# The second unit of a sigmoid gate as twelve-bit parts instead of f32, in both layers of a two-part transformer block

## The chip, the cores and the metric

The kernel runs on one core of a Trainium2 chip. The metric is the device time of one execution in microseconds; the runs before the change have a median of 2667.6 us (three runs, 2666.95 to 2668.16).

## The reference, cut to what matters

The input is one sequence of 256 tokens with 1024 channels, in f32. The first block has two layers; each ends in the second of two feed-forwards, to which an embedding term is added behind a gate. A second block with attention and 32 experts follows. The change lies in the line that computes `ple`, and moves work of the line under it.

```python
for i in range(DEPTH):                                  # DEPTH = 2, ALPHA = 4 ** 0.25
    x = layer_norm(ALPHA * x + 0.5 * swiglu(x, ffn1_up[i], ffn1_down[i]), ln1_g[i], ln1_b[i])
    mix = token_mix(x, w_in[i], ...)
    x = layer_norm(ALPHA * x + mix, ln2_g[i], ln2_b[i])
    ple = jax.nn.sigmoid(x @ w_ple_gate[i]) * (p[i] @ w_ple[i])
    x = layer_norm(ALPHA * x + 0.5 * swiglu(x, ffn2_up[i], ffn2_down[i]) + ple, ln3_g[i], ln3_b[i])
return second_block(x, ...)                             # hybrid mixer, then 32 experts, top 4
```

`w_ple_gate` is 1024 x 1024, `w_ple` is 256 x 1024, `ffn2_up` is 1024 x 5632. `swiglu(x, u, d)` splits `x @ u` into a and b and returns `(silu(a) * b) @ d`.

## The kernel before

Activations are held channels by tokens: `x` is 8 chunks of 128 channels by 256 tokens. Weights come in units of 1024 rows by 512 columns (2 MB, two DMAs), which SyncE loads into the two slots of `ring`. TensorE works through numbered groups, one per unit of weights. The groups alternate between two pairs of PSUM banks in `acc`, and a group opens only when its pair has been freed (`acc_free`, in `group_open`). Each engine has its own program, in a fixed order written out by hand; they meet at counting semaphores.

A unit is multiplied in one of two ways. `product` does it in f32: 8 chunks times 4 column blocks of 128, each over 256 tokens. `split_product` does seven of the eight chunks in parts. A weight w is split into a nearer part g (fp32r, twelve bits of it kept) and what is left, l, and a third operand k is made from both; the same is done to x. Three fp32r matmuls then replace one f32 matmul: g by g and l by l into `acc`, k by k into `mix`. The eighth chunk stays in f32 and goes into `mix` first, so that in each half of a unit four f32 records stand ahead of the wait for the parts (`k_ready`).

Three operations make the parts of one half (256 columns) of a unit: ScalarE writes g (`upper`, L1827), VectorE writes l and then k (`lower`, L2233 by way of the helper and L2324). g and k of a half have one place in memory each (`area_parts`, `zz_parts`), so the next unit's half can be split only when TensorE has read this one's; l lies in `ring_parts`, which has two slots like `ring`. The parts of x are made once for a feed-forward, for each half of the tokens: two ScalarE passes (`x_upper`, `x_upper_again`, L1832 and L1835) and two VectorE passes (`x_lower`, `x_sum`, L2331 and L2233). After `split_product`, ScalarE copies `mix` out (`k_summed`), and VectorE joins that copy with `acc` (`join`, L2345).

The stage around the change, in each layer, after the second layer norm:

- TensorE: first unit of the gate by token halves in f32 (`product_halves(PLEG)`, L1316), second unit with `product` (L1317), the embedding's product `p @ w_ple` as two groups (`G_PLE`, L1326), then the eleven units of the second feed-forward (`split_product(L, 1, n)`).
- ScalarE: the layer norm's last step, the four passes over x (L1987 on), the sigmoids of the gate's first unit (L1994), `upper` for both halves of the feed-forward's first unit, the sigmoids of the gate's second unit, then the feed-forward (`silus`). Each of the two blocks of sigmoids ends with `ple_gate`.
- VectorE: the passes over x, `lower` for both halves of the feed-forward's first unit (L2698), then the four multiplications of the embedding's product with the gate (`res`, L2700 on), which free the buffers of the `G_PLE` groups, one large addition (L2708), then the feed-forward (`hidden`).
- SyncE: the gate's second unit is loaded when TensorE is through with the group before the gate. The feed-forward's first unit is loaded when the gate's first is done, its second when the embedding's product is done.

Of the kernel before, what the change touches and what calls it, by code (L numbers as in the profile page):

```python
# [12 lines left out]
ACT = mybir.ActivationFunctionType  # L13
# [28 lines left out]
UP1, DOWN1, PROJ, GATE, MERGE, WOUT, PLEG, PLE, UP2, DOWN2, UNITS = 0, 11, 19, 24, 32, 34, 36, 38, 39, 50, 58  # L42
G_UP1, G_DOWN1, G_PROJ, G_GATE, G_MERGE, G_WOUT, G_PLEG, G_PLE, G_UP2, G_DOWN2, GROUPS = \
# [116 lines left out]
def mixed_blocks(nc, io):  # L160
    CC, NCONST = io["const_cols"], io["consts"].shape[1] - 2048
    ctx = ExitStack()
    with ctx:
# [59 lines left out]
        big = sb("big", [P, 32, T])  # L223
# [177 lines left out]
        k_summed = sem("k_sums_copied")  # L401
        a_joined = sem("a_joined")
# [222 lines left out]
        def bank_done(eng, L, a, b, i=0):  # L625

            eng.wait_ge(acc_done, L * (2 * GROUPS) + (2 * GROUPS + 2 * a + b + 1) + i * 4)
# [9 lines left out]
        def abank(a, b):  # L637
            return acc[:, 2 * (a % 2) + b, :]
# [32 lines left out]


        def parts_made(L, s):
            return 56 * L + (0, 32, 22)[s]

        def half_parts(L, s, n, b):
            return parts_made(L, s) + (2 * n + b + 3 if s == 1 else 2 * n + b + 1)


        def sums_made(L, s):  # L680
            return 50 * L + (0, 28, 20)[s]


        UPS = ((UP1, G_UP1), (UP2, G_UP2))

        def split_unit(s, n):
            return UPS[s][0] + n if s < 2 else (PROJ + n if n < 4 else GATE)

        def split_group(s, n):
            return UPS[s][1] + n if s < 2 else (G_PROJ + n if n < 4 else G_GATE)  # L690


# [8 lines left out]
        def kbank(a, b):  # L701
            return mix[:, 2 * (a % 2) + b, :]
# [257 lines left out]
        def _(pe):  # L960
# [5 lines left out]
            def product(L, r, a, rhs, cols, banks=((0, 1), (2, 3)), nk=DC, i=0, ready=None, uc=UC):  # L966

                group_open(pe, L, a, i)
                w = view(L, r)[:, 0:nk * uc].rearrange("p (k c) -> p k c", c=uc)
                for b, js in enumerate(banks):  # L970
                    for k in range(nk):
                        if b == 0 and k in (0, 4):
                            half_landed(pe, L, r, k // 4, i)
                        if ready is not None and b == 0:
                            ready(k)
                        for n, j in enumerate(js):
                            mm = pe.matmul(abank(a, b)[:, n * T:n * T + T], w[:, k, cols[j]:cols[j] + P], rhs(k),  # L977
                                           start=k == 0 and n == 0, stop=k == nk - 1, skip_group_check=True)
                    mm.then_inc(acc_done, 1)
# [22 lines left out]
            def split_product(L, s, u, i=0):  # L1002

                r, a = split_unit(s, u), split_group(s, u)
                K, wg, wk, xg, xl, xk = PARTS[s]
                group_open(pe, L, a, i)
                w, wl = (m[:, turn_of(L, r) % 2, :].rearrange("p (k c) -> p k c", c=UC) for m in (ring, ring_parts))
                if s == 2:
                    unit_landed(pe, L, r)
                for b in range(2):  # L1010
                    if s < 2:
                        half_landed(pe, L, r, b, i)
                    for c in range(2):
                        c0 = (2 * b + c) * P
                        for k in range(K, DC):
                            pe.matmul(kbank(a, b)[:, c * T:c * T + T], w[:, k, c0:c0 + P], x[:, k, :],  # L1016
                                      start=c == 0 and k == K, stop=False, skip_group_check=True)
                    pe.wait_ge(k_ready, half_parts(L, s, u, b) + i * 4)
                    for c in range(2):
                        c0, ts = (2 * b + c) * P, slice(c * T, c * T + T)  # L1020
                        for k in range(K):
                            pe.matmul(abank(a, b)[:, ts], wg[:, b, k, c * P:c * P + P], xg[:, k, :],  # L1022
                                      start=c == 0 and k == 0, stop=False, skip_group_check=True)
                            pe.matmul(abank(a, b)[:, ts], wl[:, k, c0:c0 + P], xl[:, k, :],  # L1024
                                      start=False, stop=k == K - 1, skip_group_check=True)
                            mm = pe.matmul(kbank(a, b)[:, ts], wk[:, b, k, c * P:c * P + P], xk[:, k, :],  # L1026
                                           start=False, stop=k == K - 1, skip_group_check=True)
                    mm.then_inc(acc_done, 1)
# [223 lines left out]
            for L in range(LAYERS):  # L1252
# [61 lines left out]
                        if h and j == 0:  # L1314
                            half_stats(L, 1, 0, 4, 8)
                product_halves(L, PLEG, G_PLEG, cols, 32, between=lambda: half_stats(L, 1, 1, 4, 8))  # L1316
                product(L, PLEG + 1, G_PLEG + 1, xs, cols)  # L1317
                pe.wait_ge(apart_landed, (L + 1) * 48)
                for hf in range(2):
                    a = G_PLE + hf  # L1320
# [475 lines left out]
        def _(act):  # L1796
# [23 lines left out]


            def upper(L, s, n, hf):
                if s == 2:
                    unit_landed(act, L, split_unit(s, n))
                else:
                    half_landed(act, L, split_unit(s, n), hf)
                act.activation(PARTS[s][1][:, hf], half_unit(L, s, n, hf, ring), ACT.Copy, scale=NEARER).then_inc(g_ready, 1)  # L1827
# [9 lines left out]
            def silus(L, s):  # L1837
                a0, S = UPS[s][1], 2 * L + s
                if S == 0:
                    x_upper(0, 0, 0)  # L1840
                    x_upper_again(0, 0)
                    upper(L, s, 1, 0)
                if s == 0:
                    x_upper(0, 1, 48 * L)
                    x_upper_again(0, 1)
                    upper(L, s, 1, 1)
                    bank_done(act, L, a0, 0)
                    act.activation(silu[:, a0 % 2], abank(a0, 0).rearrange("p (c t) -> p c t", c=2), ACT.Silu).then_inc(silu_ready, 1)
                for n in range(1 - s, 11):
                    a = a0 + n  # L1850
                    bank_done(act, L, a, 0)

                    act.wait_ge(h_ready, S * 11 + n)
                    copy(joined[0], kbank(a, 0).rearrange("p (c t) -> p c t", c=2)).then_inc(k_summed, 1)
                    if n < 10:
                        upper(L, s, n + 1, 0)
                    act.wait_ge(a_joined, 24 * L + (13 + n + 1 if s else n))
                    act.activation(silu[:, a % 2], joined[0], ACT.Silu).then_inc(silu_ready, 1)
                    bank_done(act, L, a, 1)
                    copy(joined[1], kbank(a, 1).rearrange("p (c t) -> p c t", c=2)).then_inc(k_summed, 1)  # L1860
                    if n < 10:
                        upper(L, s, n + 1, 1)
# [41 lines left out]
            for L in range(LAYERS):  # L1904
# [26 lines left out]
                k_sum(1, 1, rk)  # L1931
                k_sum(2, 0, rv)
                k_sum(2, 1, rg)
                act.wait_ge(a_joined, 24 * L + 10 + 1)
                act.activation(rg, rg, ACT.Silu)
                act.drain().then_inc(ret_g, 1)
                k_sum(3, 0, zp[:, 0, :, 16:])
# [5 lines left out]
                for b in range(2):  # L1943
                    k_sum(4, b, big[:, 2 * b:2 * b + 2, :])
                for b in range(2):
                    act.wait_ge(a_joined, 24 * L + 11 + b + 1)
                    act.activation(big[:, 2 * b:2 * b + 2, :], big[:, 2 * b:2 * b + 2, :], ACT.Sigmoid)
                act.wait_ge(s0_var, L + 1)
                act.activation(ml_std, ml_std, ACT.Sqrt).then_inc(s0_std, 1)
# [37 lines left out]
                for h in range(2):  # L1987
                    x_upper(1, h, 48 * L + 24 + 8 * h)
                    x_upper_again(1, h)
                for n in range(2):  # L1990
                    a = G_PLEG + n
                    for b in range(2):
                        bank_done(act, L, a, b)
                        g = act.activation(big[:, 4 * n + 2 * b:4 * n + 2 * b + 2, :],  # L1994
                                           abank(a, b).rearrange("p (c t) -> p c t", c=2), ACT.Sigmoid)
                    g.then_inc(acc_free[a % 2], 1)
                    act.drain().then_inc(ple_gate, 1)
                    if n == 0:
                        for hf in range(2):
                            upper(L, 1, 0, hf)  # L2000
                silus(L, 1)
                if L < LAYERS - 1:
                    layer_norm(L, 2, "ln3_g", "ln3_b")
# [224 lines left out]
        def _(v):  # L2228
# [112 lines left out]
            def join(L, s, n, b, dst):  # L2341
                a = split_group(s, n)
                bank_done(v, L, a, b)
                v.wait_ge(k_summed, sums_made(L, s) + (2 * n + b + 1 if s == 1 else 2 * n + b - 1))
                return v.scalar_tensor_tensor(out=dst, in0=abank(a, b).rearrange("p (c t) -> p c t", c=2), scalar=1.0 + 1.0 / STEP,  # L2345
                                              in1=dst, op0=ALU.mult, op1=ALU.add)

# [135 lines left out]
            for L in range(LAYERS):  # L2483
# [211 lines left out]
                    x_lower(L, 1, h, h + 1)  # L2695
                    x_sum(1, h)
                for hf in range(2):
                    lower(L, 1, 0, hf)  # L2698
                for n in range(2):
                    a = G_PLE + n  # L2700
                    v.wait_ge(ple_gate, L * 2 + (n + 1))
# [481 lines left out]
```

## Time and profile before

| | us |
|---|---|
| median of 3 runs (lowest, highest) | 2667.6 (2666.95, 2668.16) |
| span of the profiled execution | 2664.9 |
| TensorE busy, of it | 2619.3 (98%) |
| VectorE busy | 1116.4 (42%) |
| ScalarE busy | 676.8 (25%) |

The profiled execution's span is 2.7 us under the median of the runs. The profile is of one core. Busy times count matmuls, activations and vector operations; a matmul's end is modelled, and consecutive matmuls overlap, so starts are read rather than durations. The two layers lie at about 30 to 720 us and 720 to 1435 us, the second block's mixer up to about 1740 us, and its experts from there. The gate's second unit begins at 498.5 us in the first layer and 1208.3 us in the second.

### The profile page before, as it was taken

Reading aid. Unit: us, or ns where it says so; the run is one execution under the profiler, and the core shown is the slowest. Engines: PE = TensorE matmul, PEld = TensorE weight load, DVE = VectorE, ACT = ScalarE, POOL = GpSimd, SP = SyncE. Lnnn points to the kernel's source line nnn. Section 1 sums busy time; section 2 is a strip of 40 time slices with the busy share of each in tenths; the row PEclk is TensorE's granted clock in tenths of the full one; section 3 lists DMA queues with packets and bytes.
Section 4 is the critical chain, followed back from the end, with each engine's and each line's share of the span. In section 5 each row is a group of like instructions: output and inputs, shape, how many; then the busy total and the mean of one; then the engine's idle time right before and its main releaser. Section 6 shows DMA issues by size and latency. Waiting matters only on the chain.

```text
span 2664.9 us, 37976 instructions
## 1 busy us (share of the span) xinstructions
PE 2619.3 (98%) x15345; PEld 1912.6 (72%) x15345; DVE 1116.4 (42%) x1589; ACT 676.8 (25%) x1201; POOL 73.5 (3%) x95
## 2 busy tenths in 40 slices
PE   7999999999999999999999999999999999999998
PEld 7999888999999998899989888843333333333333
DVE  5875524586587473156832144321212212112212
ACT  3313320342143042214413043121212121112111
POOL 0000200000100110000001000000000000000000
PEclk9999999999999999999999999999999999999999
DMA  6575333456755842344562643689999999999999
GB/s 229 182 264 205 127 127 142 145 182 205 246 181 175 308 168 96 138 161 143 181 216 97 218 153 141 264 349 427 427 428 428 427 427 428 427 427 428 428 427 414
DMA packets 265072, 705.25 MB, mean 265 GB/s; under 512 B 12932, under 2 KB 155216, under 8 KB 214928
## 3 DMA queue, kind: packets, MB, share of 16 engines
q1 hardware_dynamic: 254464, 664.71, 64.7%
q0 software_dynamic: 9856, 36.41, 3.8%
q10 hardware_dynamic: 656, 2.78, 0.3%
q8 instruction: 69, 1.13, 0.2%
q14 instruction: 27, 0.22, 0.0%
HBM read 699.61 MB, written 6.60 MB: 265 GB/s over the span
## 4 chain that ended last, share of the span: by engine, by line
PE 83%; DMA 9%; SPq 7%; issue 1%; DVE 0%; ACT 0%; DVEq 0%
PE acc L977 12%; PE acc L1065 11%; PE acc L1684 11%; PE acc L1022 6%; PE mix L1026 6%; PE acc L1024 6%; SPq L862 4%; PE acc L1699 4%; PE acc L1504 4%; PE mix L1016 4%; PE acc L994 3%; DMA zp<-in_w 3%; SPq L859 3%; PE acc L1296 2%; DMA big<-in_w 2%; DMA ring<-in_w 2%
## 5 line engine op out<-in xcount | busy, mean ns | idle before, releaser
L1022 PE MATMUL acc<-branch_parts,area_parts 128*128 128x256 f32 x1176 | 344.2, 293 | 0.1
L1026 PE MATMUL mix<-big_parts,zz_parts 128*128 128x256 f32 x1176 | 332.9, 283 | 0.0
L1024 PE MATMUL acc<-area_parts,ring_parts 128*128 128x256 f32 x1176 | 332.5, 283 | 0.0
L1065 PE MATMUL acc<-big,ring 128*128 128x256 f32 (+1 forms) x1408 | 269.7, 353 | 0.0
L1065 PEld LDWEIGHTS acc<-big,ring 128*128 128x128 f32 x1408 | 241.1, 190 | 28.3 <-issue 0.8
L2982 DVE COPY zz<-acc 128x512 f32<-128x512 f32 x32 | 22.1, 692 | 548.8 <-PE acc L1684 548.8
L1022 PEld LDWEIGHTS acc<-branch_parts,area_parts 128*128 128x128 f32 x1176 | 225.1, 191 | 8.9 <-DVE zz_parts L2324 0.5
L1024 PEld LDWEIGHTS acc<-area_parts,ring_parts 128*128 128x128 f32 x1176 | 225.2, 191 | 0.2
L1026 PEld LDWEIGHTS mix<-big_parts,zz_parts 128*128 128x128 f32 x1176 | 225.1, 191 | 0.0
L977 PE MATMUL acc<-x,ring 128*128 128x256 f32 x1024 | 224.3, 380 | 0.0
L977 PEld LDWEIGHTS acc<-x,ring 128*128 128x128 f32 x1024 | 193.8, 190 | 26.7 <-issue 0.3
L2233 DVE TENSOR_TENSOR ring_parts<-ring,area_parts 128x1792 fp32r<-128x1792 f32 x84 | 170.1, 2025 | 48.8 <-ACT area_parts L1827 43.7
L2324 DVE SCALAR_TENSOR_TENSOR zz_parts<-area_parts,ring_parts 128x1792 fp32r<-128x1792 f32 x84 | 170.2, 2026 | 6.3
L1827 ACT ACTIVATE area_parts<-ring 128x1792 fp32r<-128x1792 f32 x84 | 142.3, 1694 | 12.6 <-DMA ring<-in_ffn_up 12.6
L1819 ACT ACTIVATE area<-acc 128x256 f32<-128x256 f32 (+1 forms) x66 | 32.5, 492 | 368.8 <-PE acc L1636 342.8
L1684 PE MATMUL acc<-ring,zz 128*64 128x512 f32 x512 | 117.6, 598 | 5.0 <-DMA ring<-in_w 5.0
L1016 PE MATMUL mix<-x,ring 128*128 128x256 f32 x464 | 116.8, 379 | 0.0
L994 PE MATMUL acc<-x,ring 128*128 128x128 f32 x768 | 90.5, 280 | 16.2 <-DMA ring<-in_ffn_up 16.2
L1684 PE MATMUL acc<-big,zz 128*64 128x512 f32 x432 | 100.8, 596 | 2.8 <-DMA big<-in_w 2.8
L994 PEld LDWEIGHTS acc<-x,ring 128*128 128x128 f32 x768 | 89.9, 197 | 16.4 <-issue 16.1
L1819 ACT ACTIVATE zz<-acc 128x512 f32<-128x512 f32 x66 | 39.3, 597 | 244.5 <-PE acc L1684 196.7
L2233 DVE TENSOR_TENSOR area<-area 128x256 f32<-128x256 f32 (+3 forms) x142 | 62.1, 457 | 79.0 <-PE acc L1699 68.5
(516 smaller groups left out, 3761.2 us busy)
## 6 DMA issues: line engine op xcount, KB each, us to landing
big<-in_w SPq DMA_DIRECT2D x89, 1024.0 KB, 25.6
ring<-in_ffn_up SPq DMA_DIRECT2D x88, 1024.0 KB, 5.0
ring<-in_w SPq DMA_DIRECT2D x84, 1024.0 KB, 25.7
ring<-in_w_in SPq DMA_DIRECT2D x72, 1024.0 KB, 7.1
spare<-in_w SPq DMA_DIRECT2D x42, 1024.0 KB, 25.8
area<-in_w_ada POOLq DMA_DIRECT2D x24, 1024.0 KB, 8.1
tables<-in_w SPq DMA_DIRECT2D x23, 1024.0 KB, 25.6
branch<-in_w SPq DMA_DIRECT2D x23, 1024.0 KB, 25.7
```

The costliest lines, as they stand in the source:

```text
L862: sp.dma_start(wbuf[n].unsqueeze(1), w2[:, bass.ds(e * 4 + k, 1), :]).then_inc(BUFFERS[n][0], 16)
L977: mm = pe.matmul(abank(a, b)[:, n * T:n * T + T], w[:, k, cols[j]:cols[j] + P], rhs(k), start=k == 0 and n == 0, stop=k == nk - 1, skip_gr ...
L994: mm = pe.matmul(abank(a, j // 2)[:, c0:c0 + P], w[:, k, cols[j]:cols[j] + P], x[:, k, half(h)], start=k == 0 and j % 2 == 0, stop=k == DC ...
L1016: pe.matmul(kbank(a, b)[:, c * T:c * T + T], w[:, k, c0:c0 + P], x[:, k, :], start=c == 0 and k == K, stop=False, skip_group_check=True)
L1022: pe.matmul(abank(a, b)[:, ts], wg[:, b, k, c * P:c * P + P], xg[:, k, :], start=c == 0 and k == 0, stop=False, skip_group_check=True)
L1024: pe.matmul(abank(a, b)[:, ts], wl[:, k, c0:c0 + P], xl[:, k, :], start=False, stop=k == K - 1, skip_group_check=True)
L1026: mm = pe.matmul(kbank(a, b)[:, ts], wk[:, b, k, c * P:c * P + P], xk[:, k, :], start=False, stop=k == K - 1, skip_group_check=True)
L1065: mm = pe.matmul(outs[c], w[:, k, c * P:c * P + P], rhs(kk), start=opens[c] and kk == 0, stop=kk == FC - 1, skip_group_check=not all(opens))
L1684: mm = pe.matmul(H_BANK[j // 2][lo:lo + 64, :], x_slot[:, k, :], w[:, j * UC:j * UC + UC], start=k == 0, stop=k == DC - 1)
L1827: act.activation(PARTS[s][1][:, hf], half_unit(L, s, n, hf, ring), ACT.Copy, scale=NEARER).then_inc(g_ready, 1)
L2233: return v.tensor_tensor(out, a, b, op)
L2324: v.scalar_tensor_tensor(out=PARTS[s][2][:, hf], in0=g, scalar=-1.0 / STEP, in1=l.bitcast(F32), op0=ALU.mult, op1=ALU.add) \
```

## The change

The gate's second unit becomes `split_product(L, 1, -1)`: unit -1 of the second feed-forward's stage, with that stage's parts of x. ScalarE makes its nearer parts (`upper(L, 1, -1, hf)`) right after the passes over x, ahead of the sigmoids of the first unit. VectorE makes the lower ones where it made those of the feed-forward's first unit. Its result is copied out by ScalarE, joined by VectorE, and only then put through the sigmoid. The parts of the feed-forward's first unit are made one half at a time, after each half of the gate's unit has been copied (ScalarE) or joined (VectorE). The semaphore counts move by two per layer. No DMA is added or moved.

```diff
         def half_parts(L, s, n, b):
-            return parts_made(L, s) + (2 * n + b + 3 if s == 1 else 2 * n + b + 1)
+            return parts_made(L, s) + (2 * n + b + 5 if s == 1 else 2 * n + b + 1)
...
         def split_unit(s, n):
+            if (s, n) == (1, -1):
+                return PLEG + 1
...
         def split_group(s, n):
+            if (s, n) == (1, -1):
+                return G_PLEG + 1
...
                 product_halves(L, PLEG, G_PLEG, cols, 32, between=lambda: half_stats(L, 1, 1, 4, 8))
-                product(L, PLEG + 1, G_PLEG + 1, xs, cols)
+                split_product(L, 1, -1)
...
                     x_upper(1, h, 48 * L + 24 + 8 * h)
                     x_upper_again(1, h)
-                for n in range(2):
-                    a = G_PLEG + n
-                    for b in range(2):
-                        bank_done(act, L, a, b)
-                        g = act.activation(big[:, 4 * n + 2 * b:4 * n + 2 * b + 2, :],
-                                           abank(a, b).rearrange("p (c t) -> p c t", c=2), ACT.Sigmoid)
-                    g.then_inc(acc_free[a % 2], 1)
-                    act.drain().then_inc(ple_gate, 1)
-                    if n == 0:
-                        for hf in range(2):
-                            upper(L, 1, 0, hf)
+                for hf in range(2):
+                    upper(L, 1, -1, hf)
+                a = G_PLEG
+                for b in range(2):
+                    bank_done(act, L, a, b)
+                    g = act.activation(big[:, 2 * b:2 * b + 2, :], abank(a, b).rearrange("p (c t) -> p c t", c=2), ACT.Sigmoid)
+                g.then_inc(acc_free[a % 2], 1)
+                act.drain().then_inc(ple_gate, 1)
+                a = G_PLEG + 1
+                for b in range(2):
+                    bank_done(act, L, a, b)
+                    copy(big[:, 4 + 2 * b:6 + 2 * b, :], kbank(a, b).rearrange("p (c t) -> p c t", c=2)).then_inc(k_summed, 1)
+                    upper(L, 1, 0, b)
+                for b in range(2):
+                    act.wait_ge(a_joined, 26 * L + 13 + b + 1)
+                    act.activation(big[:, 4 + 2 * b:6 + 2 * b, :], big[:, 4 + 2 * b:6 + 2 * b, :], ACT.Sigmoid)
+                act.drain().then_inc(ple_gate, 1)
                 silus(L, 1)
...
                 for hf in range(2):
-                    lower(L, 1, 0, hf)
+                    lower(L, 1, -1, hf)
+                for b in range(2):
+                    o = join(L, 1, -1, b, big[:, 4 + 2 * b:6 + 2 * b, :])
+                    if b:
+                        o.then_inc(acc_free[(G_PLEG + 1) % 2], 1)
+                    v.drain().then_inc(a_joined, 1)
+                    lower(L, 1, 0, b)
                 for n in range(2):
                     a = G_PLE + n
                     v.wait_ge(ple_gate, L * 2 + (n + 1))
```

## Rows read from the trace of the kernel before

**Rows 1.** The page: busy time of the engines, and the chain by engine

```profile
PE 2619.3 (98%) x15345; PEld 1912.6 (72%) x15345; DVE 1116.4 (42%) x1589; ACT 676.8 (25%) x1201; POOL 73.5 (3%) x95
PE 83%; DMA 9%; SPq 7%; issue 1%; DVE 0%; ACT 0%; DVEq 0%
```

**Rows 2.** Waits of TensorE, 0 to 1400 us: total, times, longest

```profile
PE acc L994 <- DMA ring<-in_ffn_up: 16.2, 1, 16.2
```

**Rows 3.** Windows: stretch, busy time of each engine, clock, DMA share, GB/s

```profile
498.50:512.30 13.80, 13.80 (x66) 12.17 (x66) 7.27 (x5) 4.76 (x5) 0.00 (x0) 1.00 0.44 152
...
1246.80:1258.60 11.80, 11.80 (x94) 11.47 (x93) 10.18 (x8) 4.89 (x5) 0.00 (x0) 1.00 0.53 178
```

**Rows 4.** Waits of SyncE's queue, 1650 to 2665 us

```profile
SPq L862 <- PE acc L1684: 80.3, 41, 4.7
```

**Rows 5.** Timeline of TensorE (start, us, engine, line, operation), both layers

```profile
498.54 13.98 PE L977 MATMUL acc<-x,ring 128*128 128x256 f32 x64
512.36 7.07 PE L1326 MATMUL acc<-ptile,zp 128*128 128x256 f32 x32
519.26 1.03 PE L1016 MATMUL mix<-x,ring 128*128 128x256 f32 x4
519.94 0.47 PE L1022 MATMUL acc<-branch_parts,area_parts 128*128 128x256 f32 x1
520.25 0.28 PE L1024 MATMUL acc<-area_parts,ring_parts 128*128 128x256 f32 x1
...
525.15 1.03 PE L1016 MATMUL mix<-x,ring 128*128 128x256 f32 x4
...
1208.30 13.98 PE L977 MATMUL acc<-x,ring 128*128 128x256 f32 x64
1222.11 7.07 PE L1326 MATMUL acc<-ptile,zp 128*128 128x256 f32 x32
```

**Rows 6.** Timeline of VectorE in the second feed-forward

```profile
529.67 2.03 DVE L2324 SCALAR_TENSOR_TENSOR zz_parts<-area_parts,ring_parts 128x1792 fp32r<-128x1792 f32 x1
...
1247.61 0.69 DVE L2345 SCALAR_TENSOR_TENSOR big<-acc,big 128x512 f32<-128x512 f32 x1 [0.18 <-ACT big L1819]
...
1259.42 0.69 DVE L2345 SCALAR_TENSOR_TENSOR big<-acc,big 128x512 f32<-128x512 f32 x1 [0.18 <-ACT big L1819]
```

**Rows 7.** ScalarE: last pass over x (timeline), and the page's row of nearer parts

```profile
495.32 0.93 ACT L1835 ACTIVATE big_parts<-x 128x896 fp32r<-128x896 f32 x1
...
L1827 ACT ACTIVATE area_parts<-ring 128x1792 fp32r<-128x1792 f32 x84 | 142.3, 1694 | 12.6 <-DMA ring<-in_ffn_up 12.6
```

**Rows 8.** DMA in 40 slices of 480 to 497 us, busy tenths

```profile
DMA  0000001088499999999999400000000000000000
```

**Rows 9.** Timeline of VectorE ahead of the second feed-forward, both layers

```profile
497.94 1.09 DVE L2233 TENSOR_TENSOR big_parts<-branch_parts,area_parts 128x896 fp32r<-128x896 f32 x1
...
505.42 2.03 DVE L2233 TENSOR_TENSOR ring_parts<-ring,area_parts 128x1792 fp32r<-128x1792 f32 x1 [6.38 <-ACT area_parts L1827]
507.52 2.03 DVE L2324 SCALAR_TENSOR_TENSOR zz_parts<-area_parts,ring_parts 128x1792 fp32r<-128x1792 f32 x1
509.46 2.02 DVE L2233 TENSOR_TENSOR ring_parts<-ring,area_parts 128x1792 fp32r<-128x1792 f32 x1
...
514.35 0.69 DVE L2233 TENSOR_TENSOR res<-acc,big 128x512 f32<-128x512 f32 x1 [0.77 <-PE acc L1326]
...
520.25 2.29 DVE L2708 SCALAR_TENSOR_TENSOR res<-res,x 128x2048 f32<-128x2048 f32 x1
...
1208.07 1.09 DVE L2233 TENSOR_TENSOR big_parts<-branch_parts,area_parts 128x896 fp32r<-128x896 f32 x1
```

**Rows 10.** Windows with the clock below 1.00, and at the kernel's start

```profile
1720.00:1732.00 12.00, 12.00 (x58) 10.92 (x58) 0.00 (x0) 1.08 (x2) 0.00 (x0) 0.72 1.01 425
...
16.00:20.00 4.00, 3.82 (x18) 3.85 (x19) 0.00 (x0) 2.09 (x2) 0.00 (x0) 1.00 1.13 420
...
24.00:28.00 4.00, 4.00 (x38) 4.00 (x38) 3.92 (x3) 2.04 (x3) 0.00 (x0) 1.00 0.52 205
```

More of the change, by code:

```diff
@@ L673, in parts_made @@
         def parts_made(L, s):
-            return 56 * L + (0, 32, 22)[s]
+            return 58 * L + (0, 32, 22)[s]
         def half_parts(L, s, n, b):
-            return parts_made(L, s) + (2 * n + b + 3 if s == 1 else 2 * n + b + 1)
+            return parts_made(L, s) + (2 * n + b + 5 if s == 1 else 2 * n + b + 1)
         def sums_made(L, s):
-            return 50 * L + (0, 28, 20)[s]
+            return 52 * L + (0, 28, 20)[s]
         UPS = ((UP1, G_UP1), (UP2, G_UP2))
         def split_unit(s, n):
+            if (s, n) == (1, -1):
+                return PLEG + 1
             return UPS[s][0] + n if s < 2 else (PROJ + n if n < 4 else GATE)
         def split_group(s, n):
+            if (s, n) == (1, -1):
+                return G_PLEG + 1
             return UPS[s][1] + n if s < 2 else (G_PROJ + n if n < 4 else G_GATE)
@@ L1007, in split_product @@
                 w, wl = (m[:, turn_of(L, r) % 2, :].rearrange("p (k c) -> p k c", c=UC) for m in (ring, ring_parts))
-                if s == 2:
+                whole = s == 2 or u == -1
+                if whole:
                     unit_landed(pe, L, r)
                 for b in range(2):
-                    if s < 2:
+                    if not whole:
                         half_landed(pe, L, r, b, i)
@@ L1822, in upper @@
             def upper(L, s, n, hf):
-                if s == 2:
+                if s == 2 or n == -1:
                     unit_landed(act, L, split_unit(s, n))
@@ L1856, in silus @@
                         upper(L, s, n + 1, 0)
-                    act.wait_ge(a_joined, 24 * L + (13 + n + 1 if s else n))
+                    act.wait_ge(a_joined, 26 * L + (15 + n + 1 if s else n))
                     act.activation(silu[:, a % 2], joined[0], ACT.Silu).then_inc(silu_ready, 1)
@@ L1933, in _ @@
                 k_sum(2, 1, rg)
-                act.wait_ge(a_joined, 24 * L + 10 + 1)
+                act.wait_ge(a_joined, 26 * L + 10 + 1)
                 act.activation(rg, rg, ACT.Silu)
@@ L1945, in _ @@
                 for b in range(2):
-                    act.wait_ge(a_joined, 24 * L + 11 + b + 1)
+                    act.wait_ge(a_joined, 26 * L + 11 + b + 1)
                     act.activation(big[:, 2 * b:2 * b + 2, :], big[:, 2 * b:2 * b + 2, :], ACT.Sigmoid)
@@ L2343, in join @@
                 bank_done(v, L, a, b)
-                v.wait_ge(k_summed, sums_made(L, s) + (2 * n + b + 1 if s == 1 else 2 * n + b - 1))
+                v.wait_ge(k_summed, sums_made(L, s) + (2 * n + b + 3 if s == 1 else 2 * n + b - 1))
                 return v.scalar_tensor_tensor(out=dst, in0=abank(a, b).rearrange("p (c t) -> p c t", c=2), scalar=1.0 + 1.0 / STEP,
```

## The prediction

> **What bounds the kernel now.** I read the page's busy shares and its chain first: TensorE is busy 98% of the span and carries 83% of the chain [rows 1]. That doesn't say that every stage is TensorE's, so I read its waits next. Up to 1400 us, which holds both layers with this stage, there is one, the 16.2 us for the first weights [rows 2]. Then the windows of the stage itself: beside the gate's second unit TensorE is busy for all of 13.80 us at a granted clock of 1.00, while VectorE works 7.27 us and ScalarE 4.76; in a unit of the second feed-forward TensorE is busy all the time too [rows 3]. So time taken from TensorE here is taken from the whole, and every pause given to it is added. After 1650 us the expert weights stream; SyncE issues them when TensorE lets it, and waited 80.3 us for it at one line alone [rows 4]. I therefore pass a shift of the layers to the end one to one.
>
> **What the change saves.** It touches one unit in each of two layers. In the plain form the unit is 64 records (each f32 matmul of 256 columns leaves two), from 498.54 to the next group at 512.36: 13.82 us, and 13.81 in the second layer (1208.30 to 1222.11) [rows 5]. In the parts form, a unit of the second feed-forward has the same shape (512 columns, seven of eight chunks as three matmuls each, the eighth in f32). Two like joins stand at 1247.61 and 1259.42: 11.81 us per unit [rows 6], without a pause of TensorE [rows 3]. The saving is 13.81 - 11.81 = 2.00 us per layer, 4.0 in all, if the parts are there when TensorE asks.
>
> **When the parts are there.** The parts of x were made before too, and at the same place, so they cost nothing new; they only become urgent. In layer 0 ScalarE ends its four passes over x at 495.32 + 0.93 = 496.25 and then makes the nearer part of each half of the unit, 1.69 us each [rows 7]: the first is there at 497.9. The unit's weights don't hold it, as the transfers end in slice 24 of 40 of that window, at 490 us [rows 8]. VectorE starts its last pass over x at 497.94 (1.09 us). Operations that don't depend on each other overlap by 0.09 (507.52 + 2.03 against 509.46), so the first lower part begins at 498.95, and the two passes for one half take 507.52 + 2.03 - 505.42 = 4.13 us [rows 9]: the first half's parts are ready at 503.08. TensorE begins the unit at 498.54; four f32 records of the eighth chunk keep it for 0.68 us (519.26 to 519.94) [rows 5], so it asks at 499.22. With 0.1 us for the semaphore and the weight load it goes on at 503.2. In an undisturbed half, the first two part matmuls are 0.31 us apart (519.94 to 520.25) [rows 5] where an even share of 11.81 us leaves about 0.12; the 0.19 falls into the pause. **First pause: 503.2 - 499.22 - 0.19 = 3.8 us.** In layer 1 VectorE's last pass starts at 1208.07 [rows 9], so the parts are ready at 1213.2; TensorE asks at 1208.30 + 0.68 = 1208.98; pause 4.15 us. The second half's parts are ready 4.04 us after the first's (505.42 to 509.46 [rows 9]), at 507.1; TensorE gets to them only near 503.2 + 5.0 + 0.9 = 509: no pause there. I take these values and not zero, because each term is a row of the same instruction on data of the same size; I allow 0.3 us either way for the release.
>
> **What is late after it.** The parts of the second feed-forward's first unit used to be made beside the gate's second unit (from 505.42 on [rows 9]). Now they can start only when the halves of that unit are read, because the nearer and the lowest parts lie in the same memory. Call E the moment when TensorE goes from the unit to the embedding's product. In the feed-forward, a half of a unit is over when the next f32 group begins at 525.15 [rows 5]; copy, nearer part and lower parts of the half that takes its place are done at 529.67 + 2.03 = 531.70 [rows 6], 6.55 us later. So VectorE is at this until E + 6.55. Only then does it come to the embedding's multiplications, which stand behind it in its order. Two of them (0.69 us each [rows 9], overlapped by 0.09) free the buffer at E + 7.9. TensorE has done the embedding's product at E + 6.90 (512.36 to 519.26) [rows 5] and needs that buffer for the feed-forward's first unit. **Second pause: with 0.15 us of release and weight load, E + 8.05 - 6.90 = 1.15 us**, the same in both layers. Behind the late work on VectorE stands also the large addition of 2.29 us [rows 9]: two more multiplications, then it, until about E + 11.6, ahead of the feed-forward's first join near E + 14.8. It costs nothing; if that cover of 3 us were gone, the join would be late by what is missing. ScalarE's sigmoids of the second unit, now behind a join, end about E + 4, before VectorE needs them. Its sigmoids of the first unit come 3.4 us later, at about 502, and the buffer that they free is asked for only after the whole unit: hidden. SyncE's queue is not moved; its next feed-forward loads wait for the same groups and shift with them.
>
> **Sum.** Layer 0: 3.8 + 1.15 - 2.0 = +2.95. Layer 1: 4.15 + 1.15 - 2.0 = +3.3. Together **+6.2 us**: a span of 2664.9 + 6.2 = 2671.1. The runs' median is 2.7 us over the profiled span, so 2667.6 + 6.2 = 2673.8. What this can't price is TensorE's clock after such a pause: apart from the start, no row has it idle for about 4 us. Bounds from the nearest rows: nothing on one side (the feed-forward runs at 1.00 [rows 3]); on the other, the stretch from 1720 to 1732 has a mean clock of 0.72, so 12 x 0.28 / 0.5 = 6.7 us at 1.2 GHz instead of 2.4, which is 3.4 us lost, though a run of small matmuls stood before it and no pause [rows 10]. After the first 16.2 us of idling [rows 2], TensorE left 18 records in 4 us where it later left 38 [rows 10]. I take nothing, as a pause of 4 us is nearer to none than to 16, and keep 3.4 per pause for the range.
>
> The Trainium skill, TensorE: Matmul & The Clock Gate, section "Part 1: The HAM clock gate (the "warmup" mystery)", states that an idle array falls back to half clock until it has been busy again. The kernel's start agrees with it (18 records against 38); the drop near 1725 us came without idling and isn't covered by it. By this rule the long pauses would each be followed by a slow stretch, and the time would be the fourth rival's.
>
> **The rivals.**
> 1. *The parts come in time* (faster). Both pauses would be gone and the full 4.0 us kept: 2663.6. It decides at 499.22 us: VectorE would have to end the first half's lower part 3.9 us earlier. Nothing in the rows lets it, as its pass over x starts late, behind ScalarE's four. Chance 0.03.
> 2. *The second pause is not there* (within 0.2%). It hangs on the order of VectorE's work; if it can free the buffer before E + 6.75, 3.8 + 4.15 - 4.0 = +3.95 stays: 2671.6. Against it, the multiplications stand behind both lower parts in the code. Chance 0.15.
> 3. *The delay is absorbed.* If the expert stream ran from a point that doesn't move with TensorE, up to all 6.2 us would vanish: 2667.6. Against it stand SyncE's waits for TensorE [rows 4]. Chance 0.05.
> 4. *The clock falls* in one of the long pauses: +3.4 gives 2677.2, in both 2680.6. For it speaks the start, against it that 4 us is short. Chance 0.25.
>
> **How the numbers follow.** The forecast, 2673.8 (2672.8 to 2674.8 by the release times), has 0.50; 0.02 is left for gains that I don't see. A measurement of this kernel can tell 0.2%, 5.3 us, from no change. Faster: 0.03 + 0.02 = 0.05. Within: 0.15 + 0.05, and 0.01 of the forecast, 0.21. Slower: 0.74. The range takes in the missing second pause (2671.6, less 0.6) and one fall of the clock (2677.2, with 1 for the spread): 2671.0 to 2678.2. It leaves out the clock falling twice and full absorption.
>
> **What would show it.** In the profile of the changed kernel, TensorE's waits before 1400 us should hold two of 3.5 to 4.3 us for VectorE's second lower pass (the line that writes zz_parts), ahead of the gate's second unit's parts; two of about 1 us for VectorE's res, ahead of the feed-forward's first unit; and the unit itself, pause taken off, should take 11.8 us. The granted clock behind these pauses tells rival 4. I am wrong if the parts matmuls begin before 502 us in layer 0, if the feed-forward's first unit follows the embedding's product without a gap, or if the layers end 6 us later and the span doesn't.

## The result, and the profile after

| | before | after |
|---|---|---|
| median of 5 runs, us | 2667.6 | 2678.5 |
| lowest, highest | 2666.95, 2668.16 | 2677.19, 2679.9 |
| span of the profiled execution | 2664.9 | 2675.4 |

The change made the kernel slower by 10.9 us; the ratio is 1.0041, with a 95% interval of 1.0031 to 1.0052. The forecast was +6.2 us, with a range up to 2678.2. The sign was right, the time is just outside the range.

TensorE's waits up to 1450 us, after (total, times, longest); before, the first line was the only one [rows 2]:

```profile
PE acc L998 <- DMA ring<-in_ffn_up: 16.1, 1, 16.1
PE acc L1027 <- DVE zz_parts L2335: 7.1, 2, 3.6
PE mix L1021 <- DVE res L2244: 1.4, 2, 0.7
PE acc L1027 <- DVE big_parts L2335: 0.4, 1, 0.4
PE mix L1109 <- ACT zz L1873: 0.3, 1, 0.3
```

Each line names the tile that TensorE was about to write and read from, and what it waited for. Lines two and three are the two forecast pauses, once in each layer. The last two lines belong to neither; they stand between the two stages. The timeline of TensorE through the stage, in the first layer and then in the second, to be held against [rows 5]:

```profile
498.34 1.03 PE L1021 MATMUL mix<-x,ring 128*128 128x256 f32 x4
502.92 0.43 PE L1027 MATMUL acc<-branch_parts,area_parts 128*128 128x256 f32 x1 [3.56 <-DVE zz_parts L2335]
503.15 0.41 PE L1029 MATMUL acc<-area_parts,ring_parts 128*128 128x256 f32 x1
503.36 0.41 PE L1031 MATMUL mix<-big_parts,zz_parts 128*128 128x256 f32 x1
...
515.45 7.07 PE L1331 MATMUL acc<-ptile,zp 128*128 128x256 f32 x32
523.24 1.13 PE L1021 MATMUL mix<-x,ring 128*128 128x256 f32 x4 [0.72 <-DVE res L2244]
...
1213.04 1.03 PE L1021 MATMUL mix<-x,ring 128*128 128x256 f32 x4
1217.61 0.58 PE L1027 MATMUL acc<-branch_parts,area_parts 128*128 128x256 f32 x1 [3.54 <-DVE zz_parts L2335]
...
1231.14 7.07 PE L1331 MATMUL acc<-ptile,zp 128*128 128x256 f32 x32
1238.93 1.13 PE L1021 MATMUL mix<-x,ring 128*128 128x256 f32 x4 [0.72 <-DVE res L2244]
```

Read the starts. The parts' matmuls begin at 502.92, where the forecast had 503.2. But the matmuls after the pause start 0.23 and then 0.21 us apart, where the same instructions in an undisturbed half of the kernel before start 0.12 apart:

```profile
520.36 0.28 PE L1026 MATMUL mix<-big_parts,zz_parts 128*128 128x256 f32 x1
520.48 0.28 PE L1022 MATMUL acc<-branch_parts,area_parts 128*128 128x256 f32 x1
```

The unit takes 515.45 - 498.34 = 17.11 us in the first layer and 18.10 in the second, in place of 13.82. Part of that is the pause, and the rest is the clock, as the windows of after show (the last number but two is the granted clock; the first window is the pause itself, the next two follow the pauses):

```profile
498.30:502.90 4.60, 1.06 (x6) 0.61 (x5) 4.53 (x4) 3.29 (x4) 0.00 (x0) 1.00 0.70 226
502.90:506.90 4.00, 3.98 (x20) 3.98 (x21) 3.92 (x2) 0.00 (x0) 0.00 (x0) 0.57 0.75 265
1217.60:1223.60 6.00, 5.99 (x29) 5.99 (x30) 3.92 (x2) 0.00 (x0) 0.00 (x0) 0.52 0.49 174
```

TensorE counts as busy throughout the second and third window, with a record count of 20 in 4 us where an undisturbed window of a split unit has 94 in 11.8 us, 32 in 4 [rows 3]. The granted clock was 0.57 and 0.52 there: TensorE ran at 1.2 GHz, half of its full 2.4, for most of both.

**A measure for the stage.** For each kernel I take the time from the first matmul behind the gate's first unit to ScalarE's copy of the second half of the feed-forward's first unit. Before, that is 531.25 - 498.54 = 32.7 us in the first layer, and 1241.01 - 1208.30 = 32.71 in the second. The rows on ScalarE's side, before and after:

```profile
531.25 0.60 ACT L1819 ACTIVATE area<-mix 128x512 f32<-128x512 f32 x1 [1.77 <-PE mix L1026]
...
1241.01 0.60 ACT L1819 ACTIVATE area<-mix 128x512 f32<-128x512 f32 x1 [1.77 <-PE mix L1026]
```

```profile
535.35 0.60 ACT L1824 ACTIVATE area<-mix 128x512 f32<-128x512 f32 x1 [1.77 <-PE mix L1031]
...
1251.02 0.60 ACT L1824 ACTIVATE area<-mix 128x512 f32<-128x512 f32 x1 [1.77 <-PE mix L1031]
```

After, it is 535.35 - 498.34 = 37.01 us and 1251.02 - 1213.04 = 37.98: +4.3 and +5.3, so 9.6 of the 10.5 us by which the spans differ. Of the rest, 0.64 lies between the two stages (the small waits above) and 0.5 behind 1251 us, less 0.2 before the first stage.

### The profile page after: what moved, and what is told of

Its sections match the earlier page's. It is cut to its first block, busy times and chain, and to the rows that moved or that the text cites. A ratio compares the mean times of both kernels' runs of the same rounds, so it can differ in the third digit from the quotient of the medians.

```text
span 2675.4 us, 38124 instructions
## 1 busy us (share of the span) xinstructions
PE 2620.4 (98%) x15401; PEld 1914.8 (72%) x15401; DVE 1134.2 (42%) x1601; ACT 684.8 (26%) x1209; POOL 73.5 (3%) x95
## 3 DMA queue, kind: packets, MB, share of 16 engines
q8 instruction: 70, 1.15, 0.2%
## 4 chain that ended last, share of the span: by engine, by line
PE 82%; DMA 9%; SPq 6%; DVE 1%; ACT 1%; issue 1%; DVEq 0%; ACTq 0%
PE acc L1070 11%; PE acc L1689 11%; PE acc L981 11%; PE acc L1027 6%; PE mix L1031 6%; PE acc L1029 6%; PE acc L1704 4%; PE acc L1509 4%; PE mix L1021 4%; SPq L866 3%; DMA zp<-in_w 3%; PE acc L998 2%; PE acc L1301 2%; DMA big<-in_w 2%; DMA ring<-in_w 2%; SPq L863 2%
## 5 line engine op out<-in xcount | busy, mean ns | idle before, releaser
L1027 PE MATMUL acc<-branch_parts,area_parts 128*128 128x256 f32 x1232 | 362.5, 294 | 7.1 <-DVE zz_parts L2335 7.1
L1031 PE MATMUL mix<-big_parts,zz_parts 128*128 128x256 f32 x1232 | 350.4, 284 | 0.0
L1029 PE MATMUL acc<-area_parts,ring_parts 128*128 128x256 f32 x1232 | 350.3, 284 | 0.0
L1027 PEld LDWEIGHTS acc<-branch_parts,area_parts 128*128 128x128 f32 x1232 | 237.6, 193 | 16.5 <-DVE zz_parts L2335 7.9
L1029 PEld LDWEIGHTS acc<-area_parts,ring_parts 128*128 128x128 f32 x1232 | 237.8, 193 | 0.2
L1031 PEld LDWEIGHTS mix<-big_parts,zz_parts 128*128 128x128 f32 x1232 | 237.7, 193 | 0.0
L981 PE MATMUL acc<-x,ring 128*128 128x256 f32 x896 | 196.3, 380 | 0.0
L2244 DVE TENSOR_TENSOR ring_parts<-ring,area_parts 128x1792 fp32r<-128x1792 f32 x88 | 178.2, 2025 | 39.9 <-ACT area_parts L1832 34.7
L981 PEld LDWEIGHTS acc<-x,ring 128*128 128x128 f32 x896 | 169.6, 190 | 23.5 <-issue 0.3
L2335 DVE SCALAR_TENSOR_TENSOR zz_parts<-area_parts,ring_parts 128x1792 fp32r<-128x1792 f32 x88 | 178.2, 2025 | 6.6
L998 PEld LDWEIGHTS acc<-x,ring 128*128 128x128 f32 x768 | 89.8, 197 | 16.3 <-issue 16.0
```

The lines of the kernel that those rows point to most:

```text
L998: mm = pe.matmul(abank(a, j // 2)[:, c0:c0 + P], w[:, k, cols[j]:cols[j] + P], x[:, k, half(h)], start=k == 0 and j % 2 == 0, stop=k == DC ...
L2244: return v.tensor_tensor(out, a, b, op)
L2335: v.scalar_tensor_tensor(out=PARTS[s][2][:, hf], in0=g, scalar=-1.0 / STEP, in1=l.bitcast(F32), op0=ALU.mult, op1=ALU.add) \
```

## The experiments

Theory A: the two pauses are what the forecast says, and what it left out is the clock, which falls behind the first pause of each layer whatever work follows. Theory B: the parts' matmuls are slow at this place for a reason of their own, for instance because VectorE writes operands of the next half beside them. Medians are over the kernel before on the same chip; "stage" is the measure above; "slow" is a stretch with the granted clock near 0.5, "full" one with 1.00.

| kernel | over before, us | ratio (95%) | stage, layer 0 and 1, us | stretch behind the first pause |
|---|---|---|---|---|
| changed | +10.9 | 1.0041 (1.0031 to 1.0052) | 37.0, 38.0 | slow, slow |
| changed, again | +9.8 | 1.0041 (1.0027 to 1.0054) | 36.9, 37.9 | slow, slow |
| eight fillers | +5.2 | 1.0019 (1.0010 to 1.0028) | 35.5, 35.5 | full |
| four fillers | +6.1 | 1.0024 (1.0015 to 1.0034) | 35.5, 35.5 | full |
| multiplications inside | +7.0 | 1.0027 (1.0016 to 1.0039) | 37.0, 36.0 | slow, slow |
| early passes | +1.4 | 1.0006 (0.9997 to 1.0015) | 33.5, 33.5 | full |
| reordered | -3.8 | 0.9989 (0.9980 to 0.9998) | 31.1, 31.1 | full (0.4 us of pause left) |
| reordered, early passes | -3.3 | 0.9989 (0.9979 to 0.9998) | 30.7, 30.7 | full (no pause) |
| before, paused | +11.6 | 1.0043 (1.0029 to 1.0057) | (35.9, 34.3) | slow, slow |

The stage of the paused kernel is counted from the end of its pause.

### The changed kernel again

> The changed kernel once more, on the same chip as the next three. Both theories: 2677 to 2680 us, about 10.9 us over the kernel before. If the granted clock is the cause of the spread of its times, then the length of its slow stretches changes from one profile to the next (3.4 and 6.8 us in the first).

It came out at 2677.65 us, 9.8 over. Its profile has the same two long waits (7.1 us, two times), and slow stretches of the same lengths as in the first profile, so of the expectation only the level was met here; the lengths didn't change. In the run with the multiplications inside, below, the longer stretch is in the other layer.

### Fillers in the pause

```diff
+                    if (s, u, b) == (1, -1, 0):
+                        for _ in range(8):
+                            pe.matmul(abank(a, 0)[:, 0:T], const("ones"), consts[:, 0:T], start=True, stop=True)
                     pe.wait_ge(k_ready, half_parts(L, s, u, b) + i * 4)
```

> The changed kernel, with eight useless f32 matmuls (256 columns, 0.43 us each, 3.5 us in all) in the first pause of each layer; their result is overwritten by the parts. Theory A, the clock: nothing is gained by ending the wait, but TensorE is not idle, the granted clock stays at 1.00 behind the wait, and the 1.7 and 2.9 us that the two slow stretches cost come back: 4.6 us under the changed kernel, about 5.9 over the kernel before. Theory B, the parts matmuls themselves are slow at this place (their operands are being written): no change, about 10.9 over.

Measured: 2673.07, 5.2 over the kernel before (expected 5.9). Nothing useful was added and the parts come no earlier, yet 4.6 us are gone. Four in place of eight:

> The same with four useless matmuls (1.7 us), which leaves TensorE idle for about 2.2 us in layer 0 and 2.5 in layer 1. If only the whole pause of nearly 4 us lets the clock fall: as with eight, about 5.9 us over the kernel before. If any idle time of this kind does: still 10.9 over. If by chance of phase: between them, with times that spread.

Measured: 2674.03, 6.1 over. The window behind the shorter pause, in the second layer, with the matmul that ended it:

```profile
1215.04 0.39 PE L1030 MATMUL acc<-branch_parts,area_parts 128*128 128x256 f32 x1 [1.82 <-DVE zz_parts L2338]
```

```profile
1215.00:1219.00 4.00, 3.96 (x33) 3.96 (x34) 3.93 (x2) 0.00 (x0) 0.00 (x0) 1.00 0.76 269
```

33 records in 4 us, clock 1.00, and VectorE is as busy beside it (3.93 of 4.00 us) as in the slow window of the changed kernel (3.92). That speaks against theory B: the same matmuls, on the same operands, beside the same writes, run at full rate. The stage is 35.5 us in both layers and in both kernels, so 37.0 and 38.0 minus 35.5 is the price of the clock in the profile of after: **1.5 and 2.5 us**.

### The second pause

```diff
                 tt(l, w, g, ALU.subtract)
+                if between is not None:
+                    between()                       # the first two multiplications into res
                 v.drain()
...
+                    lower(L, 1, 0, b, between=(lambda: gated(0)) if b else None)
```

> The changed kernel, with the embedding's first two multiplications moved between the two lower passes of the feed-forward's first unit (second half). The step on trial is that the second pause comes from their place in VectorE's order. If so, TensorE's waits for res (0.7 us, with weight load 0.89 between groups, in each layer) are gone, and it is 1.8 us under the changed kernel, about 9.1 over the kernel before, with the first pause and the slow clock as they were. Rival: the buffer is freed late by something else (the join, the sigmoids), and the wait stays: 10.9 over.

Measured: 7.0 over the kernel before, 2.8 us under the changed kernel on this chip (expected 1.8; the medians' spread covers the difference). TensorE's waits before 1450 us:

```profile
PE acc L1027 <- DVE zz_parts L2337: 7.1, 2, 3.5
PE mix L1109 <- ACT zz L1873: 0.3, 1, 0.3
PE acc L1027 <- DVE big_parts L2337: 0.2, 1, 0.2
```

The wait for res is gone. In this profile the short slow stretch is in the second layer, where the changed kernel has it in the first: 36.01 against 37.01, so the second pause cost **1.0 us** in each layer (forecast 1.15). The rival, a buffer held by something else, falls.

### A shorter first pause

```diff
                     if h and n != 1:
                         x_upper_again(2 if n == 0 else 0, 0)
+                    if h and n == 1:
+                        x_upper(1, 0, 48 * L + 24)
+                        x_upper_again(1, 0)
...
-                for h in range(2):
-                    x_upper(1, h, 48 * L + 24 + 8 * h)
-                    x_upper_again(1, h)
+                x_upper(1, 1, 48 * L + 32)
+                x_upper_again(1, 1)
```

> The changed kernel, with ScalarE's two passes over the first half of the tokens moved into the layer norm, behind its squares, where ScalarE idles. VectorE can then do its first two passes at once after the norm (491.5 instead of 494.6 us), and the first half's parts are ready about 2 us earlier: first pause 1.6 us in layer 0 and 2.0 in layer 1 instead of 3.6 and 3.6. Theory A (clock falls only behind the long pause): 4.0 us of pause and 4.6 of slow clock gone, about 2.3 over the kernel before. If the clock falls behind a pause of 2 us too: about 6.9 over.

Measured: 2669.17, 1.4 over (expected about 2.3). The wait is 1.53 us in the second layer, and the window behind it is at full clock:

```profile
1210.67 0.39 PE L1027 MATMUL acc<-branch_parts,area_parts 128*128 128x256 f32 x1 [1.53 <-DVE zz_parts L2337]
```

```profile
1210.70:1214.70 4.00, 4.00 (x33) 4.00 (x34) 3.88 (x2) 0.00 (x0) 0.00 (x0) 1.00 1.09 387
```

Moving two ScalarE passes of 0.93 us each took 2.0 us off each pause and, with it, the clock's price.

### Useful work in the pause

```diff
                 product_halves(L, PLEG, G_PLEG, cols, 32, between=lambda: half_stats(L, 1, 1, 4, 8))
-                split_product(L, 1, -1)
                 pe.wait_ge(apart_landed, (L + 1) * 48)
                 for hf in range(2):
-                    a = G_PLE + hf
+                    if hf:
+                        split_product(L, 1, -1)
+                    a = G_PLEG + 1 + 2 * hf
...
+                gated(0)                            # the first two multiplications into res
                 for b in range(2):
                     o = join(L, 1, -1, b, big[:, 4 + 2 * b:6 + 2 * b, :])
...
+                gated(1)
```

> The changed kernel, with the first of the two groups of the embedding's product (3.45 us) put ahead of the gate's second unit, and its multiplications ahead of that unit's join. It fills the first pause with work that is needed anyway, and the feed-forward's first unit now waits for the unit's join and no longer for the multiplications. First pause about 0.4 us in layer 0 and 0.8 in layer 1, no second pause, clock at 1.00: 1.2 - 4.0 = 2.8 us under the kernel before, 2664.8. If the saving of 2.0 per unit isn't real, it is level with the kernel before or over it.

Measured: 2664.01, 3.8 us under the kernel before (expected 2.8), with an interval (0.9980 to 0.9998) that ends just below 1. The stage is 31.07 us in both layers, 1.64 under before. The profile lists no wait for the parts, but a short one is left: the first of their matmuls follows the four f32 records after 1.13 us, not 0.68.

```profile
500.67 1.03 PE L1021 MATMUL mix<-x,ring 128*128 128x256 f32 x4
501.80 0.39 PE L1027 MATMUL acc<-branch_parts,area_parts 128*128 128x256 f32 x1
```

With the early passes as well:

> Both of the last two together. No pause is left in the stage, and the whole saving shows: 4.0 us under the kernel before, 2663.6. If it stands no lower than with the reordering alone, the remaining pause was hidden or the saving is smaller than 2.0 per unit.

Measured: 2664.49, 3.3 under (expected 4.0). The median is no lower than with the reordering alone, so by the medians neither the rest of the pause nor the full saving can be seen; the stages differ by 0.37 us a layer, less than the runs' spread. The traces do tell them apart: the stage is 30.70 us, without a wait of TensorE in it (the last two waits are the small ones between the stages).

```profile
1205.68 3.62 PE L1332 MATMUL acc<-ptile,zp 128*128 128x256 f32 x16
1209.13 1.03 PE L1021 MATMUL mix<-x,ring 128*128 128x256 f32 x4
1209.81 0.47 PE L1027 MATMUL acc<-branch_parts,area_parts 128*128 128x256 f32 x1
1210.12 0.28 PE L1029 MATMUL acc<-area_parts,ring_parts 128*128 128x256 f32 x1
...
1236.38 0.60 ACT L1825 ACTIVATE area<-mix 128x512 f32<-128x512 f32 x1 [1.77 <-PE mix L1031]
```

```profile
PE acc L1027 <- DVE big_parts L2338: 0.3, 1, 0.3
PE mix L1109 <- ACT zz L1874: 0.3, 1, 0.3
```

Here the parts' matmuls follow the four f32 records after 0.68 us, as in an undisturbed half [rows 5]. 32.71 - 30.70 = **2.01 us per layer is the saving itself** (forecast 2.00).

### The pause without the change

The kernel before, with VectorE's last pass over x repeated, and TensorE made to wait for it ahead of the unsplit unit:

```diff
-                    x_sum(1, h)
+                    x_sum(1, h, 3 * h)                  # three more times for h = 1
...
+                pe.wait_ge(k_ready, parts_made(L, 1) + 2)
                 product(L, PLEG + 1, G_PLEG + 1, xs, cols)
```

> The kernel before, unsplit, with a pause at the same place: VectorE repeats its last pass over x three times (1.1 us each) and TensorE waits for it ahead of the gate's second unit. From 499.03 + 3 x 1.17 = 502.5 us it follows that TensorE pauses for about 3.7 us net in layer 0 and 4.1 in layer 1, 7.8 together, with no fp32r matmul and no part of the weights near it. Theory A (a pause of nearly 4 us lets the clock fall, whatever follows): 7.8 plus 3 to 7 us of loss at half clock, 11 to 15 over the kernel before, and the windows behind the pauses show a granted clock of about 0.5. Theory B (the fall belongs to the parts matmuls): 7.8 over, clock at 1.00.

Measured: 2679.0, 11.6 over the kernel before, where the pauses alone are 7.8. The waits, the windows behind them, and the ends of the stage:

```profile
PE acc L977 <- DVE big_parts L2234: 7.8, 2, 3.9
```

```profile
500.70:506.70 6.00, 6.00 (x14) 4.83 (x15) 3.06 (x2) 3.39 (x2) 0.00 (x0) 0.50 0.60 210
1217.20:1221.20 4.00, 4.00 (x12) 3.29 (x13) 1.25 (x1) 2.02 (x2) 0.00 (x0) 0.62 0.87 307
```

```profile
500.67 17.13 PE L977 MATMUL acc<-x,ring 128*128 128x256 f32 x64 [3.88 <-DVE big_parts L2234]
1217.17 15.59 PE L977 MATMUL acc<-x,ring 128*128 128x256 f32 x64 [3.88 <-DVE big_parts L2234]
...
536.54 0.60 ACT L1820 ACTIVATE area<-mix 128x512 f32<-128x512 f32 x1 [1.77 <-PE mix L1026]
1251.50 0.60 ACT L1820 ACTIVATE area<-mix 128x512 f32<-128x512 f32 x1 [1.77 <-PE mix L1026]
```

f32 matmuls run at 1.2 GHz behind such a pause too: 14 records in 6 us, where a unit in f32 leaves 66 in 13.8 [rows 3]. Counted from the end of the pause, the stage takes 35.87 and 34.33 us instead of 32.71, so the clock took 3.2 and 1.6 us. Theory B falls with this.

### The kernel before again

> The kernel before once more, for its trace on this chip: both theories expect about 2667.7 us. It tells whether the small wait for big_parts (0.4 us) in the second layer's projections, which the changed kernel shows and the first trace of before doesn't, comes with the change.

One run, 2665.4 us. Its trace has only the first wait for DMA before 1450 us, and so has the paused kernel's but for its two pauses. The 0.3 us for the squares at about 1198 us comes in all seven kernels with the split unit and in none of the three traces without it, so it comes with the change; why is open. The wait for big_parts is another matter. It follows the weights of that half, which land at different times in different profiles. The two extremes, with the issue of the weights at 953.56 us in the kernel with the early passes and at 956.05 in the one with eight fillers:

```profile
962.69 1.49 ACT L1832 ACTIVATE big_parts<-ring 128x1536 fp32r<-128x1536 f32 x1 [2.49 <-DMA ring<-in_w_in]
```

```profile
963.77 1.49 ACT L1835 ACTIVATE big_parts<-ring 128x1536 fp32r<-128x1536 f32 x1 [1.07 <-DMA ring<-in_w_in]
```

ScalarE starts on them 9.13 us after the issue in the first, and TensorE waits 0.52 us; in the second it starts after 7.72, and TensorE doesn't wait. In the four profiles where it starts within 8.2 us (both of before, the paused kernel, eight fillers) there is no such wait; in the seven where it takes 8.87 to 9.13 us the wait is 0.25 to 0.52. What delays the weights is open, and as eight fillers are on the other side, the delay can't be put down to the split unit alone.

## Why the prediction was wrong where it was

- **The saving.** Forecast 2.00 us per layer, found 2.01 with no pause left in the stage. Right.
- **The first pause.** Forecast 3.8 and 4.15 us. The stage is 35.50 with the clock kept up; less 30.70 and the second pause of 1.0, the first pause is 3.8 us in both layers. Right in the first layer. In the second, 0.35 was too much. Before, TensorE began the unit 0.60 us after VectorE's last pass over x in the first layer and 0.23 after it in the second [rows 5, 9], and the forecast kept that lead of 0.37 us. After, it is 0.60 and 0.61: most of the lead (0.28) went in the wait for the squares. The 0.1 us of release in the sum stood on no row; VectorE's pass (L2335) ended at 502.87 and TensorE went on at 502.92.
- **The second pause.** Forecast 1.15, found 1.0 (its 0.15 us for release and weight load stood on no row either). The mechanism holds: it went when the multiplications went ahead in VectorE's order.
- **What is hidden.** The late large addition, the sigmoids and SyncE's loads cost nothing that the waits show. Right.
- **One to one to the end.** The spans differ by 10.5 us, the stages by 9.6. Right, to the 0.9 us that the small waits and the last part add.
- **The clock: the step that failed.** The sum took it at nothing, "as a pause of 4 us is nearer to none than to 16". It fell behind all eight pauses of 3.5 to 3.9 us of which I have a trace (the changed kernel twice, the multiplications inside, the pauses in the kernel before; two layers each), and behind none of the four of 1.5 and 1.8 us. In the profile of after it cost 1.5 and 2.5 us. With these two, the forecast's own sum gives 6.2 + 4.0 = 10.2 against 10.9 measured. With the measured terms, 2 x (3.8 + 1.0 - 2.01) + 4.0 = 9.6, which is what the two stages grew by.

The fourth rival had the mechanism, and even the case that came, both pauses, but at 3.4 us each it was priced too high (2680.6), and the range left it out. The price came from a stretch that amounts to 6.7 us at 1.2 GHz. Behind the pauses it is as long only in one layer of each profile, and part of it can fall into the pause, where it costs nothing (the last window below, in the changed kernel's second profile, ends before TensorE goes on at 1216.33, and has a clock of 0.73). And parts' matmuls that start 0.213 instead of 0.12 us apart lose 0.44 of such a stretch, not half: 3.4 x 0.44 = 1.5. In the profile of after, 10 x 0.17 / 0.5 = 3.4 us in the first layer and 11 x 0.31 / 0.5 = 6.8 in the second; with the multiplications inside, 6.8 and then 3.5:

```profile
498.00:508.00 10.00, 6.44 (x39) 5.99 (x38) 8.75 (x5) 3.59 (x4) 0.00 (x0) 0.83 0.62 210
1213.00:1224.00 11.00, 7.46 (x38) 7.00 (x38) 8.44 (x5) 3.29 (x4) 0.00 (x0) 0.69 0.57 191
```

```profile
498.00:508.00 10.00, 6.45 (x33) 6.35 (x33) 7.48 (x4) 2.35 (x3) 0.00 (x0) 0.66 0.63 210
1213.00:1224.00 11.00, 7.95 (x50) 7.84 (x51) 7.30 (x5) 2.87 (x5) 0.00 (x0) 0.84 0.53 187
```

```profile
1214.00:1216.00 2.00, 0.00 (x0) 0.00 (x0) 1.93 (x2) 1.03 (x2) 0.00 (x0) 0.73 1.07 377
```

Two errors lie in leaving it out. The choice between the bounds was made by the distance between durations, which says nothing about a thing that has two states. And the two layers have the same pause, so if the clock falls in one it is likely to fall in the other: "once" should have had less chance than "both". The rule of the Trainium skill that was weighed (TensorE: Matmul & The Clock Gate, Part 1, an idle array falls back to half clock until it has been busy again) was the better guide here: by it, the long pauses are each followed by a slow stretch, and the traces agree with 8 of 8. As put here it doesn't set the four short pauses apart, behind which the clock stayed at 1.00. The prediction's own sign for the rule was also weaker than it says: the row of the kernel's start that has 18 records prints a granted clock of 1.00 [rows 10], so there only the count of records speaks for half speed.

The price varies between executions: 1.5 and 2.5 us in one profile, 2.5 and 1.5 in the run with the multiplications inside, 3.2 and 1.6 in the paused kernel. It doesn't explain how far the times of one kernel lie apart, though. The five times of after span 2.7 us and those of before only 1.2, but on the chip of most experiments 22 runs of the kernel before, without a pause, span 4.0 us, and the 11 with eight fillers, whose profile has no slow stretch in the two stages, span 5.3. What spreads them is open. A candidate that no run tests is the other slow stretch, near 1725 us [rows 10], which comes to about 3 us at 1.2 GHz in the profile of the reordered kernel (a mean clock of 0.97 from 1700 to 1750 us) and to about 7 in the other ten (0.93).

## What to carry to other kernels

A cheaper form of a matmul saves only what its operands' preparation lets it: before moving a stage to such a form, write down when the last operand is ready and when TensorE asks, and look for work that can stand between (here half of an independent product, which turned +9.8 us into -3.8 on one chip). Count a pause of TensorE not by its length alone but also by what the clock does behind it, and where the same pause occurs several times, let it fall in all of them. Where one memory is shared by the parts of consecutive units, moving a unit into the scheme moves the next unit's preparation behind it, and whatever stands after that in the engine's order.

## What the runs showed of the hardware

Fillers that do nothing useful made the kernel 4.6 us faster (2677.65 to 2673.07 on one chip); with them the granted clock stayed at 1.00 behind the pauses. Four of them (1.7 us of work, 1.8 us of waiting left) did nearly as well as eight: 2674.03. One fp32r matmul over 256 columns takes 0.12 us of TensorE's time, half an f32 one 0.216 (13.82 us for 64 records), at a granted clock of 1.00; behind the pause, at 1.2 GHz, the former took 0.21.
